# Reordering and re-placing work in a two-block kernel: query weights in pieces among gathered rows, more homes for them, attention outputs without turning

## What is computed

```python
xn = rmsnorm_2(h, norm1_g)
q_a, k_a, v_a, q_b, k_b, v_b, gate_a, gate_b = split(xn @ w_in)
y_a = merge(moba_attention(q_a, k_a, v_a)) @ w_out_moba        # 8 heads, softmax with ALiBi
y_b = merge(stick_breaking_attention(q_b, k_b, v_b)) @ w_out_sb  # 8 heads
h = h + (sigmoid(gate_a) * y_a + sigmoid(gate_b) * y_b) @ w_mix_out
h = h + peer_ffn(rmsnorm_2(h, norm2_g), w_q, sub_keys, expert_u, expert_v)
return rmsnorm_2(h, final_norm_g)
```

## Time and profile before

| | us |
|---|---|
| median of 3 runs | 1801.35 (1800.93 to 1805.69) |
| the profiled execution | 1801.28 |
| its span, first to last instruction | 1799.5 |
| layer 1, layer 2, second block to the first gather, gathers to the end | about 470, 440, 215, 675 |

### The profile page before, as it was taken

One profiled execution on the slowest core, in us unless ns is written; L12 is line 12 of the kernel. 1 busy time (PEld: TensorE's weight loads), 2 busy tenths in 40 slices (PEclk: granted clock), 3 DMA queues, 4 the chain that ended last, 5 costly groups with the idle time before them and its releaser, 6 DMA issues.

```text
span 1799.5 us, 22611 instructions
## 1 busy us (share of the span) xinstructions
PE 1630.4 (91%) x8816; PEld 1229.1 (68%) x8816; DVE 1127.5 (63%) x1993; ACT 848.3 (47%) x1570; POOL 354.8 (20%) x368
## 2 busy tenths in 40 slices
PE   6999999999999999999989998889998777777786
PEld 5998998999898899899879997544443222222232
DVE  4747765555665776655554556677766667676754
ACT  4555634444455553544455544345444444444343
POOL 0100000000020000000040000444446434444440
PEclk9999999999999999999999999899999999999999
DMA  6533354555543346455534342999999999999996
GB/s 247 193 119 141 140 202 170 190 187 188 193 164 123 136 170 216 164 188 188 188 139 153 141 164 94 392 415 420 422 421 422 422 421 422 422 421 421 421 422 264
DMA packets 67066, 464.51 MB, mean 258 GB/s; under 512 B 7440, under 2 KB 9616, under 8 KB 11536
## 3 DMA queue, kind: packets, MB, share of 16 engines
q0 software_dynamic: 36864, 268.45, 35.9%
q1 hardware_dynamic: 29808, 194.29, 30.1%
q10 hardware_dynamic: 288, 0.33, 0.1%
HBM read 462.00 MB, written 1.05 MB: 257 GB/s over the span
## 4 chain that ended last, share of the span: by engine, by line
PE 64%; DMA 20%; DVE 6%; ACT 4%; issue 4%; POOL 3%; SPq 0%; POOLq 0%; ACTq 0%; DVEq 0%
PE acc L529 14%; PE acc L530 14%; PE acc L531 14%; DMA row_w_lo<-in_peer_uv,arena 12%; DMA arena<-in_peer_uv,arena 4%; PE acc L1597 4%; PE acc L1600 3%; DMA row_w_hi<-in_peer_uv,arena 3%; PE att L531 3%; PE att L530 3%; PE att L529 3%; DVE w_lo L525 1%; POOL arena L2157 1%; ACT w_hi L519 1%; ACT gate_raw L1723 1%
## 5 line engine op out<-in xcount | busy, mean ns | idle before, releaser
L525 DVE TENSOR_TENSOR w_lo<-arena,w_hi 128x2048 fp32r<-128x2048 f32 x176 | 404.6, 2300 | 232.1 <-ACT w_hi L519 231.7
L519 ACT CAST w_hi<-arena 128x2048 fp32r<-128x2048 f32 x176 | 335.4, 1908 | 147.7 <-PE acc L531 136.3
L529 PE MATMUL acc<-xa_hi,w_hi 128*128 128x256 f32 x928 | 266.9, 288 | 0.0
L530 PE MATMUL acc<-xa_hi,w_lo 128*128 128x256 f32 x928 | 263.7, 284 | 0.0
L531 PE MATMUL acc<-xa_lo,w_hi 128*128 128x256 f32 x928 | 263.6, 284 | 0.0
L1715 ACT ACTIVATE arena<-arena 128x1 f32<-128x1 f32 x256 | 51.8, 202 | 302.8 <-DVE arena L1995 122.9
L1995 DVE SCALAR_TENSOR_TENSOR arena<-arena 128x1024 f32<-128x1024 f32 x106 | 129.7, 1226 | 92.0 <-DMA arena<-in_peer_uv,arena 91.9
L529 PEld LDWEIGHTS acc<-xa_hi,w_hi 128*128 128x128 f32 x928 | 179.1, 193 | 4.0 <-issue 3.1
L530 PEld LDWEIGHTS acc<-xa_hi,w_lo 128*128 128x128 f32 x928 | 179.1, 193 | 0.2
L531 PEld LDWEIGHTS acc<-xa_lo,w_hi 128*128 128x128 f32 x928 | 179.0, 193 | 0.0
L2157 POOL DMA_INDIRECT arena<-in_peer_uv,arena x106 | 120.6, 1137 | 143.2 <-PE acc L1600 119.0
(11 more groups left out here) (296 smaller groups left out, 3346.6 us busy)
## 6 DMA issues: line engine op xcount, KB each, us to landing
arena<-in_units SPq DMA_DIRECT2D x176, 1024.0 KB, 4.8
arena<-in_bias SPq DMA_DIRECT2D x1, 2048.0 KB, 9.2
arena<-in_peer_uv,arena POOLq DMA_INDIRECT x106, 15.6
x_res<-in_x SPq DMA_DIRECT2D x2, 512.0 KB, 4.2
arena<-in_norm_mix_g SPq DMA_DIRECT2D x2, 512.0 KB, 6.7
arena<-in_norm_mlp_g SPq DMA_DIRECT2D x2, 512.0 KB, 6.6
arena<-in_norm_g SPq DMA_DIRECT2D x2, 512.0 KB, 6.4
arena<-in_final_norm_g SPq DMA_DIRECT2D x2, 512.0 KB, 9.6
```

What stands on the lines that cost most here:

```text
L519: nc.scalar.copy(w_hi[:, s, :], raw[s]).then_inc(S["hi_ready"], 1)
L525: nc.vector.tensor_tensor(w_lo[:, s, :], raw[s], w_hi[:, s, :].bitcast(F32), ALU.subtract).then_inc(S["lo_ready"], 1)
L529: nc.tensor.matmul(out_, lh, rh, start=first, stop=False)
L530: nc.tensor.matmul(out_, ll, rh, start=False, stop=False)
```

## The change

It has four parts.

- Layers: `num_squares` moves from `mo 0` to `mo 2`, `num_scale` from `mo 1` to `mo 2`; VectorE makes `ha_take` and `logits` ahead of `take`.
- Second attention: transposes and product of a step come one step later (between the halves of the unit two after its scores, and behind that unit). The softmax weights are multiplied with one over their sum ahead of the transposes. The product is written transposed, so that ScalarE and VectorE split each pair directly into what `yab` reads; `turn_y` and `y_take` are gone. The norm's row of `mix` has another address, and it and the last norm's row are loaded in front of `mix 0`.
- Query units: 5, 6 and 7 have raw homes of their own, and SP issues them in the order 0, 1, 2, 5, 6, 7, 3, 4, each when its own home is free. TensorE makes a query in eight pieces of six matmuls, one in front of each of eight items.
- Ring: 17 places, taken by longest disuse, that open by item number: 5 at item 0, then one each at items 5, 6, 20, 30, 40 and 50 (the raw homes of queries 2 to 7, each after its `split_lo`), six more at item 72. Ordering semaphores of the routing are merged into one.

```diff
-EARLY, LATE, EARLY_ITEMS = 8, 8, 88
-QUERIES_BEFORE = {h: 4 if h == 2 else 16 * (h - 2) - 6 if h > 3 else 12 for h in range(2, P_HEADS)}
+PIECES = 8
+QUERIES_FROM = {2: 2, 3: 12, 4: 22, 5: 32, 6: 42, 7: 52}
+PLACES = 17
+OPEN_FROM = [0] * 5 + [5, 6, 20, 30, 40, 50] + [72] * 6
...
-    first = {1: 3, 2: 11}.get(g, P_TOP * (g - 2) + 4)
+    first = {1: 3, 2: 14, 3: 24}.get(g, P_TOP * (g - 2) + 4)
...
+HOME = [g % RING for g in range(QUERY0 + 5)] + [RAW_RING + i for i in range(3)]
+LAST_AT_HOME = [max((v for v in range(g) if HOME[v] == HOME[g]), default=None) for g in range(len(HOME))]
...
+        raw += [area("bias", 0, UNIT), area("bias", UNIT, UNIT), area("gb", 0, UNIT)]
...
-            if USER[g] is not None:
-                sp.wait_ge(S["lo_ready"], USER[g] + 1)
+            if LAST_AT_HOME[g] is not None:
+                sp.wait_ge(S["lo_ready"], LAST_AT_HOME[g] + 1)
...
+                if unit == ("mix", 0, "T"):
+                    sp.wait_ge(S["pair_done"], at("pair_done", STEPS[-1]))
+                    sp.dma_start(g_peer, rows_of(A["norm2_g_2"])).then_inc(S["g_loaded"], mark("g_loaded", "n2", 16))
+                    sp.dma_start(g_last, rows_of(A["final_norm_g_2"].rearrange("(o d) -> o d", o=1))).then_inc(
+                        S["g_last_loaded"], mark("g_last_loaded", 0, 16))
                     sp.wait_ge(S["x_lo"], at("x_lo", ("y2", KT - 1)))
...
-                unit_dma(sp, u)
+                if unit[0] != "pq":
+                    unit_dma(sp, u)
+            for h in (0, 1, 2, 5, 6, 7, 3, 4):
...
+                unit_dma(sp, at_unit2["pq", h])
...
                 elif (name, i) == ("mo", 0):
                     num_take(3)
+                elif (name, i) == ("mo", 2):
                     num_squares()
...
-                take(name, i)
                 if (name, i) in TURNED_WITHIN:
                     ha_take(TURNED_WITHIN[name, i])
                 if (name, i) in SCORED_AFTER:
                     logits(SCORED_AFTER[name, i])
+                take(name, i)
+                if (name, i) in SCORED_AFTER:
                     split_lo(dve, u + 3)
...
-                    c0 = 3 * P + e * DH2
-                    nc.tensor.matmul(att[2][:, c0:c0 + DH2], pT2[:, e, 0, :], v0, start=True, stop=True)
-                    second = att[3][:, c0:c0 + DH2]
-                    nc.tensor.matmul(second, pT2[:, e, 1, :], v0, start=True, stop=False)
-                    m = nc.tensor.matmul(second, pT2[:, e, 2, :], v1, start=False, stop=True)
+                    first, second = (att[2 + t][DH2 * e:DH2 * e + DH2, 3 * P:4 * P] for t in range(TT))
+                    nc.tensor.matmul(first, v0, pT2[:, e, 0, :], start=True, stop=True)
+                    nc.tensor.matmul(second, v0, pT2[:, e, 1, :], start=True, stop=False)
+                    m = nc.tensor.matmul(second, v1, pT2[:, e, 2, :], start=False, stop=True)
...
+            def query_piece(h, piece):
...
+                n_, k0 = piece // 4, 2 * (piece % 4)
+                for k in (k0, k0 + 1):
+                    m = passes(b[0][:, n_ * SEQ:(n_ + 1) * SEQ], hi[:, k, n_ * P:(n_ + 1) * P], lo[:, k, n_ * P:(n_ + 1) * P],
+                               xh[:, k, :], xl[:, k, :], k == 0, k == 7)
...
-                    if n == before:
-                        other_queries(h)
-                    elif n == before + 2:
+                    if n0 <= n < n0 + PIECES:
+                        query_piece(h, n - n0)
+                    elif n == n0 + PIECES + 1:
                         rank_keys(h)
...
+            def y_rounded(tag, p):
+                act.wait_ge(S["pair_done"], at("pair_done", (tag, p)))
+                for t in range(TT):
+                    nc.scalar.copy(xb_hi[:, n_, t * P:(t + 1) * P], att[2 + t][:, 3 * P:4 * P])
...
+            def normalise(p):
...
+                for t, (c0, c1) in enumerate(((0, P), (P, 3 * P))):
+                    nc.vector.tensor_tensor(lg2[:, :, c0:c1], lg2[:, :, c0:c1],
+                                            rinv2[:, 2 * t:2 * t + 2].unsqueeze(2).broadcast_to([P, 2, c1 - c0]), ALU.mult).then_inc(
...
             split_lo(dve, at_unit2["pq", 1])
             head_weights(0)
+            split_lo(dve, at_unit2["pq", 2])
             for n in range(ITEMS):
                 row_dot(n)
-                if n < 2:
-                    split_lo(dve, at_unit2["pq", 2 + n])
+                if n == 0:
+                    split_lo(dve, at_unit2["pq", 3])
...
-                if n == EARLY_ITEMS:
-                    pool.wait_ge(S["unit_done"], at("unit_done", ("u", at_unit2["pq", P_HEADS - 1])))
                 if USER_BEFORE[n] is not None:
                     pool.wait_ge(S["rows_multiplied"], USER_BEFORE[n] + 1)
+                elif 5 <= PLACE[n] < 11:
+                    pool.wait_ge(S["lo_ready"], QUERY0 + PLACE[n] - 5 + 2 + 1)
+                elif PLACE[n] >= 11:
+                    pool.wait_ge(S["unit_done"], at("unit_done", ("u", at_unit2["pq", P_HEADS - 1])))
```

More of the change, by code:

```diff
@@ L60, in ring_places @@
 def ring_places():
-    return [n % EARLY if n < EARLY_ITEMS else (n - EARLY_ITEMS + EARLY) % (EARLY + LATE) for n in range(ITEMS)]
+    places = []
+    for n in range(ITEMS):
+        last = {p: m for m, p in enumerate(places)}
+        places.append(min((p for p in range(PLACES) if OPEN_FROM[p] <= n), key=lambda p: (last.get(p, -1), p)))
+    return places
 PLACE = ring_places()
@@ L110 @@
     "pair_mx": "with their bias, and the largest", "pair_negm": "minus the maximum", "pair_part": "an exp",
-    "pair_probs": "all weights of a pair", "pair_rinv": "one over their sums", "odds": "the odds to stop at a key or pass it",
+    "pair_probs": "all weights of a pair", "pair_rinv": "one over their sums", "pair_scaled": "the weights times that", "odds": "the odds to stop at a key or pass it",
     "odds_masked": "without the future", "left_ready": "what is left of the stick", "pair_turned": "weights transposed, in PSUM",
     "pair_pT": "and in memory", "pair_done": "times the values", "y_part": "the first of two steps into memory",
-    "y_ready2": "a pair's output is in memory",
     "query_in": "and in memory", "query_done": "half of a tile's first queries", "half_sum": "TensorE is through with the first half of the last sum",
@@ L120 @@
     "iota": "0 .. 15", "rank_done": "scores of a head's sub-keys", "rank_ready": "in memory",
-    "top8": "the best eight", "top8_at": "where they are", "top8_out": "the scores without them", "next8": "the next eight",
-    "next8_at": "where they are", "top_f": "places as floats", "cand": "sums of the best of both halves",
-    "pos_i": "places in both halves", "pos_f": "as floats", "pick": "one-hot", "picked": "times the sub-keys' numbers",
-    "both_f": "the sub-keys' numbers", "expert_f": "the experts' numbers", "expert_ready": "as indices",
+    "routed": "a step of the routing on VectorE", "expert_ready": "the experts' numbers as indices",
     "best_diff": "scores less the largest", "best_exp": "their exp, with its sum", "wrec": "one over it",
@@ L1620, in second_pe @@
                     else:
-                        unit_t(b, s, xh, xl, 4 * (i % 2), i % 2 == 0, i % 2 == 1, ("u", u))
-                scored, pair, before = pair_at(u)
-                if pair and scored:
-                    if before:
-                        product(*before)
-                    scores(*pair)
-                elif pair:
-                    turned(*pair)
-                if (name, i) == ("gb2", 3):
-                    product(*STEPS[-1])
-                    turn_y()
-                elif (name, i) == ("mix", 0):
+                        unit_t(b, s, xh, xl, 4 * (i % 2), i % 2 == 0, i % 2 == 1, ("u", u), between)
+                if late:
+                    product(*late)
+                if fresh:
+                    scores(*fresh)
+                if (name, i) == ("mix", 0):
                     turn_keys()
@@ L2070, in second_dve @@
                 take(name, i)
-                scored, pair, before = pair_at(u)
-                if pair and scored:
-                    if before:
-                        y_take(*before)
-                    weights(*pair)
-                if (name, i) == ("gb2", 3):
-                    y_take(*STEPS[-1])
-                    turn_dve(dve, xb_hi, xb_lo, "y2", lambda k: 1.0)
-                elif (name, i) == ("mix", 3):
+                if fresh:
+                    weights(*fresh)
+                if late:
+                    y_rest(*late)
+                if (name, i) == ("mix", 3):
                     peer_norm()
```

202 lines of the change are left out of this document (105 added, 97 removed).

## The result

| | kernel before, us | changed kernel, us | ratio, 95% interval |
|---|---|---|---|
| first comparison | 1801.14 (1800.07 to 1805.69) | 1776.29 (1774.82 to 1779.47) | 0.9869, 0.9851 to 0.9886 |
| again, later | 1798.72 (1796.33 to 1801.59) | 1778.41 (1775.49 to 1780.29) | 0.9886, 0.9867 to 0.9906 |
| profiled execution (its span) | 1801.28 (1799.5) | 1774.82 (1773.1) | |

What follows compares the result with a forecast made beforehand. TensorE's chain was taken to bound the first part, the last gathered byte at 421 GB/s the second. Gains of 8.6, 5.5 and 9.7 us (11.2 less 1.5), 23.8 in all, take 1801.3 to 1777.5 us; range 1771 to 1788 us.

Steps and rivals of the forecast that it cites:

- Layers: Attention layers: TensorE's two waits and the slow clock behind them mostly go, 4.3 us a layer, 8.6 us for two.
- Second attention: Second attention: stick waits (1.9 us) and turning transposes with their waits (3.6 us) go, 5.5 us, bounds 4 to 6.
- taken as zero: Second-attention product streaming 128 columns instead of 64: no change in time; if twice as long, 10.8 us lost.
- Bytes: Gather stage: four query units and the norm's row, 4.72 MB, moved ahead of it save 11.2 us at 421 GB/s.
- What the ring costs: Gather-stage opening: fewer open places leave DMA queues idle; 1.5 us lost, between 0 and 4.
- The stall of TensorE at item 10: Gather stage: query take, cast and exponential hold ScalarE 5.7 us against 4.5 us of TensorE work; 1 to 2 us, once.
- an engine that is behind hides idle time: Gather stage: some DMA engine runs about 6 us behind; if already so in the opening, the others' idle time costs nothing.
- it fits by 4%: Gather stage: ten rows with one query unit and one ranking take TensorE 23.8 us against 24.9 us of DMA.
- B: Gather stage: an engine's latency, not bytes, sets the pace, so moving bytes gives nothing; 1787 us, chance 0.05.
- C: Layers: the moved work doesn't reach TensorE, another wait replaces the old, gain falls to 2 us; 1784 us, chance 0.10.
- D: Gather stage: clock stays at the 1.2 GHz level, a row with its piece takes 4.9 us; slower, 1825 us, chance 0.04.
- A: Gather stage starves: a 2 to 4 us burst each ten items until 30, 8 to 10 us more; 1786 us, chance 0.15.

Runs made afterwards that it cites:

- one half: Changed kernel, but both heads of a pair write their second-attention product to the same half of the partitions (second head's part left out): 1779.44 us.
- the copies back: Changed kernel with only the copies of a unit's banks (`take`) put back ahead of the logits: 1777.97 us.
- the squares back: Changed kernel with only `num_squares` put back behind `mo 0`: 1781.08 us.
- one place less: Changed kernel with one ring place less until item 20 (home of query 3 opens at item 20, not item 6): 1779.71 us.
- alternating heads: Changed kernel with the six matmuls of each second-attention product alternating between the two heads, instead of three of one and then three of the other: 1774.74 us.
- combined kernels: Changed kernel with products and scores of the second attention alternating between heads and bank copies ahead of the logits: 1775.57 us; with query 2's pieces two items later, 1772.03 us.

## Why the prediction was right, point by point

- **Layers, 8.6 us forecast, 6.9 measured in the two stretches, 5.8 up to the second block.** Layer 1 gave 4.3 as summed, layer 2 2.6. The step that failed is "the second layer shows 1.87 and 0.89 us, the same pattern": the waits are the same, but the dip of the clock, 2 us of the 4.8, stands in the earlier trace rows for layer 1 only, and I did not look at the clock of layer 2. What the dip gave back in layer 1 was lost again in another from 517 to 521 us (last section), and 0.23 us in the stretches to the third groups' scores. The attribution to the squares and the copies was half wrong as well: the 1.3 us of copies counted only because the squares had pushed everything behind them, and then, with `num_scale`, for 0.7. The second scaled tile, due 0.3 us behind TensorE, was waited for 0.33 us; for ScalarE's chain behind the squares nobody waited.
- **Second attention, 5.5 us forecast, 8.1 measured.** 1.9 for the stick waits and 3.6 for the turning are gone. The term that failed is the product "taken as zero". I compared durations over 64 and 128 columns and left out that the change gives the two heads different halves of the partitions. It gains 0.30 us a product, 2.4 us; with 1.9 and 3.6 that is 7.9 of the 8.1. The nearest row was in the earlier trace rows: the layers' product, 128*64 stationary and 256 columns, alternating between halves, makes 12 records from 148.90 to 150.34 us, 0.12 us each, as much as a matmul over half as many columns into one half costs in the run with one half. The Trainium skill, page "TensorEngine Tiling (Array Packing)", section "Performance Considerations", names swapping what stays and what streams, with column tiling, for a streamed side of 64; this trace agrees, 1.37 to 1.07 us, and 0.81 with the heads in turn, where the swap without the second half took 1.45.
- **Bytes, 11.2 us forecast.** Three of the four units were moved back and cost 6.6 to 7.0 of the 7.5 us by the byte end. The bytes carry the part; unit 3 and the norm's row were not moved back by themselves.
- **What the ring costs, 1.5 us forecast.** Byte end 657.7 less 11.2 is 646.5; measured were 648.0 and 648.4, so 1.5 to 1.9 (1.3 to 2.2 over the eight profiles). The size was right and the working only in part. The stall of TensorE at item 10, forecast at 1 to 2 us, came, once, with 2.11 us. The two gaps that I counted (1.3 and 1.5 us behind the seventh and eighth gather) didn't come: these went out 16.3 and 20.2 us behind the first gather, where I had 18.7 and 22.7 from a trace in which the split of query 2 stands behind the first row's dot; after, it lies ahead of that dot, in VectorE's 5.3 us of waiting for the row. In three profiles with the same code of the stage the opening is thin all the same (318 GB/s from 1128 to 1136 us with the copies back, where the changed kernel has 413; with the squares back and with one half 338 and 324 in the same place behind the first gather), and the byte end is within 647.8 to 648.4 there too. The reason for halving them, an engine that is behind hides idle time, is refuted by the run with one place less. What the changed kernel lost instead lies in the thin stretches behind them, the second of them behind that stall; and a row with its piece takes 2.43 us against 2.49 of DMA, which I had written down as "it fits by 4%" and which means that a short queue stays short. Pieces took no dip away: whole units do as well.
- **The sum.** By named events the change gave 5.8 + 8.1 + 9.5 = 23.4 us in the profiled execution, where 23.8 were forecast, and 7.5 instead of 9.5 in the second profile's gather stage. That it fits so closely is luck in part: the layers fell 2.8 us short, and the second attention gave 2.6 us more than summed, 2.4 of it the products, which were taken as zero. The other 3.3 us of the profiled difference lie ahead of the first window scores (below), and the tail lost 0.2. The bound of 1785 us was too tight for the forecast's own terms: the lower ones, 3.6 + 4 + 6, give 1787.7 us, still inside the stated range.
- **Rivals.** B, C and D fell (the clock was 0.96 in the stage, no row took 4.9 us). A came in part. Its sign is there: from 1146 to 1166 us the rate is 398 GB/s, under the 410 named, and the forecast's 421 GB/s from 15 us behind the first gather on was not kept. One burst of ScalarE passed on to the DMA queue, not one each ten items, and with the opening it cost about 2 us, not 8 to 10.

## What to carry over

When one wait is priced in two places, read the clock at both, and behind them: the same wait cost 4.3 us with a dip behind it and 2.6 without, and over a longer stretch a second dip took most of the difference back. Where a short queue feeds a bound engine, a producer that fits by 2% hardly refills it. Spreading the extra work evenly gained nothing here; starting it two rows later, which also took away a wait for ScalarE, gained 2.7 us. And when an edit changes which partitions matmuls write, look for a row in the same trace that already alternates halves, and price the edit by its spacing of starts.

## What was unexpected of the hardware

- **Starts out of program order.** With two heads in different halves, the second head's first matmul (L1530) started at 1041.81 us, ahead of the first head's third (L1532, at 1042.02): the records of one engine's queue are not in program order there. Spacing is 0.11 us within one half, 0.055 across halves.
- **The same code, at another clock.** The first window scores begin at 126.8 us in both runs of the changed kernel and with one place less, between 127.4 and 128.9 in five others, and at 129.8 to 130.2 in the kernel before, with the layers undone, with the squares back, with alternating heads and in two of the combined kernels, though the edits reach TensorE only behind that point. Executions of one kernel differ by as much: with alternating heads, 1773.23 us at a mean granted clock of 0.984 and 1778.27 at 0.980. The granted clock of one stretch tells them apart, here in the changed kernel and then in that with alternating heads:

```profile
60.00:90.00 30.00, 29.56 (x197) 27.12 (x196) 20.53 (x31) 16.85 (x18) 9.66 (x10) 1.00 0.38 141
```

```profile
60.00:90.00 30.00, 30.00 (x173) 27.56 (x173) 19.24 (x30) 16.12 (x18) 8.62 (x11) 0.89 0.41 144
```

  0.11 of 30 us is 3.3 us. The two profiles of the changed kernel agree in it. What sets it stays open. It is as large as many of the effects above, which is why they are read between named events and not from spans.
- **A dip behind waits in one layer only, and another far behind.** Waits of 1.1 to 1.9 us plus 0.9 were followed by 0.5 of the clock in layer 1 in all three kernels that had them, and never in layer 2. The same three have a clock of 1.00 from 500 to 530 us. The eleven profiles without these waits have no dip in layer 1, and each has one that begins between 516 and 519 us, at half the clock for 3 to 7 us, while TensorE is never idle (in the changed kernel 1.7 us of loss). Whether one dip takes the other's place, and why, no run shows; but it takes back about what the missing dip of layer 1 had given.
